# Attention with K projected for two blocks at once in the two column halves, values in groups of eight and a ring of sixteen; a two-bit search in the expert selection

## The reference, cut to what matters

```python
# attention: 8 heads, 64 + 32 columns of q and k, 64 of v
kv = (rmsnorm(c_kv, kv_norm_g) @ w_ukv).reshape(b, s, N_HEADS, QK_NOPE + V_DIM)
k = jnp.concatenate([kv[..., :QK_NOPE], broadcast(k_pe)], axis=-1)
scores = jnp.einsum('bqhd,bkhd->bhqk', qb, k)
p = jax.nn.softmax(scores, axis=-1)
o = jnp.einsum('bhqk,bkhd->bqhd', p, v)
# expert choice: each of 16 experts takes its cap best tokens of each request
aff = jax.nn.softmax(logits, axis=-1)
gates, idx = lax.top_k(aff.T, cap)          # cap = 128 (prompt), 256 (sample)
```

## Time and profile before

| | us |
|---|---|
| median of 3 runs | 4376.39 (4362.48 to 4377.37) |
| the profiled execution | 4363.99, of which span 4362.1 |
| sample attention, steady part, 600 to 1590 | 990.0, PE busy 974.8 |
| prompt attention, 1610 to 1925 | 315.0, PE busy 292.4 |
| selection, the 30 rounds, 2389.8 to 2474.0 | 84.2, DVE busy 57.7, PE 19.6 |

### The profile page before, as it was taken

The page is one execution under the profiler, slowest core; times in us unless marked ns, Lnnn a source line. Parts: engine busy times, 40 slices in busy tenths (PEclk is TensorE's granted clock), DMA queues, the critical chain, the costliest instruction groups (busy, mean ns, idle before and its releaser), DMA issues. The chain is left out here.

```text
span 4362.1 us, 53821 instructions
## 1 busy us (share of the span) xinstructions
PE 3865.6 (89%) x19385; PEld 2948.4 (68%) x19385; DVE 1752.8 (40%) x2962; ACT 1576.5 (36%) x2789; POOL 1156.4 (27%) x906
## 2 busy tenths in 40 slices
PE   7799799999999989976997259999999999999992
PEld 1799745555555534534775149999999999999991
DVE  0322144444444424345223754444444444444443
ACT  0444234444444433432222024433344333343432
POOL 0000047676767745542111130000000000000000
PEclk9899999999999989987999569999999999999996
DMA  7212300000000010024442044445444444444436
GB/s 258 99 68 74 105 4 6 7 5 8 7 8 4 6 47 10 12 91 156 150 149 95 0 136 145 145 148 159 146 144 144 144 145 154 152 144 144 144 111 250
DMA packets 296366, 428.07 MB, mean 98 GB/s; under 512 B 43558, under 2 KB 206246, under 8 KB 295050
## 3 DMA queue, kind: packets, MB, share of 16 engines
q1 hardware_dynamic: 269900, 327.41, 23.0%
q0 software_dynamic: 13824, 50.34, 5.1%
q10 hardware_dynamic: 12480, 48.24, 2.8%
HBM read 335.88 MB, written 90.06 MB: 98 GB/s over the span
## 5 line engine op out<-in xcount | busy, mean ns | idle before, releaser
L972 DVE TENSOR_REDUCE att_mx<-att_m_ps 128x1 f32<-128x512 f32 x640 | 425.3, 685 | 554.0 <-PE att_m_ps L723 554.0
L1102 POOL TENSOR_TENSOR att_acc<-att_acc,att_e 128x512 f32<-128x512 f32 x448 | 562.4, 1275 | 288.3 <-ACT att_e L917 285.6
L917 ACT ACTIVATE att_e<-att_s_ps 128x512 f32<-128x512 f32 x640 | 376.4, 595 | 614.0 <-PE att_s_ps L784 581.8
L1929 ACT ACTIVATE moe_wh<-moe_raw 128x1024 fp32r<-128x1024 f32 x384 | 373.9, 1045 | 304.7 <-DMA moe_raw<-w_up 182.0
L1976 DVE TENSOR_TENSOR moe_wl<-moe_raw,moe_wh 128x1024 fp32r<-128x1024 f32 x384 | 444.7, 1221 | 43.4 <-ACT moe_wh L1929 43.4
L1850 POOL DMA_INDIRECT s_x<-moe_ye,moe_to_add x48 | 75.8, 1580 | 1442.2 <-issue 1156.8
L1886 PE MATMUL moe_a_ps<-moe_xh,moe_wh 128*128 128x384 f32 x1024 | 350.5, 342 | 44.4 <-DVE moe_hf L2004 41.3
L1887 PE MATMUL moe_a_ps<-moe_xl,moe_wh 128*128 128x384 f32 x1024 | 347.6, 339 | 0.0
L1888 PE MATMUL moe_a_ps<-moe_xh,moe_wl 128*128 128x384 f32 x1024 | 347.6, 339 | 0.0
L1888 PE MATMUL moe_u_ps<-moe_xh,moe_wl 128*128 128x384 f32 x1024 | 342.3, 334 | 0.0
L1887 PE MATMUL moe_u_ps<-moe_xl,moe_wh 128*128 128x384 f32 x1024 | 342.2, 334 | 0.0
(11 more groups left out here) (235 smaller groups left out, 7264.1 us busy)
## 6 DMA issues: line engine op xcount, KB each, us to landing
moe_raw<-w_gate SPq DMA_DIRECT2D x64, 1024.0 KB, 5.3
moe_raw<-w_up SPq DMA_DIRECT2D x64, 1024.0 KB, 7.7
moe_raw<-w_down SPq DMA_DIRECT2D x64, 1024.0 KB, 6.7
ada_wa<-w_ada SPq DMA_DIRECT2D x12, 2048.0 KB, 9.9
s_x<-outp_x ACTq DMA_DIRECT2D x24, 512.0 KB, 5.4
s_xn<-outp_xn ACTq DMA_DIRECT2D x24, 512.0 KB, 5.9
fin_x<-s_x SPq DMA_DIRECT2D x12, 1024.0 KB, 12.1
inp_x<-x_sample SPq DMA_DIRECT2D x8, 1024.0 KB, 5.3
```

What stands on the lines that cost most here:

```text
L917: nc.scalar.activation(e[:, s % RING, :], s_ps[s % 2][:, :], ACT.Exp, scale=SCALE).then_inc(exp_done, 1)
L972: nc.vector.tensor_reduce(mx[:, u % CB, u // CB:u // CB + 1], m_ps[u % MB][:, :], AX, ALU.max).then_inc(max_part, 1)
L1102: nc.gpsimd.tensor_tensor(acc[:, b % 2, kt % 2, :], acc[:, b % 2, kt % 2, :], e[:, s % RING, :], ALU.add).then_inc(sum_done, 1)
L1929: nc.scalar.activation(wh[:, s, part, :], raw[:, s, part, :], ACT.Copy).then_inc(w_hi_done, 1)
```

## The change

Three things in attention. (1) `project_k` runs for two key blocks in one go, at every even block only: the same weights for block j into the lower and for block j+1 into the upper half of the array's columns and of the buffer. ACT then writes two pieces of `kh`, DVE two of `kl`. It stands at step 1 instead of 2, behind `values`. (2) `GROUP` is 8 instead of 4 and `RING` 16 instead of 8. (3) The prompt's step numbers of `DEN` to `OUT` now hold for the sample too, and `spread_inverses` stands right behind `values`. In selection a round settles two bits: 15 rounds, three candidates above the threshold each.

```diff
-    RING = 8
+    RING = 16
-    GROUP = 4
+    GROUP = 8
-    KSTEP = 2
-    LOW, SUM, DEN, INV, SPREAD, OUT = (3, 4, 6, 7, 9, 10) if NT == 8 else (3, 4, 8, 9, 11, 12)
+    KSTEP = 1
+    LOW, SUM, DEN, INV, SPREAD, OUT = 3, 4, 6, 7, 9, 10
...
                 for k in range(KKV):
-                    mm = nc.tensor.matmul(out[0:NOPE, :], wk[:, k0, k, :], ct_cols(KQ + k, j),
-                                          start=(k == 0), stop=(k == KKV - 1))
+                    for i in range(2):
+                        mm = nc.tensor.matmul(out[i * NOPE:(i + 1) * NOPE, :], wk[:, k0, k, :], ct_cols(KQ + k, j + i),
+                                              start=(k == 0), stop=(k == KKV - 1))
...
             for j in range(NQB):
-                if j >= 2:
-                    pe.wait_ge(k_lo_done, j - 1)
-                project_k(o_ps[j % 2], j, 0)
+                if j % 2 == 0:
+                    project_k(o_ps[j // 2], j, 0)
...
                     scores(hp, s)
-                    if kt == KSTEP and project:
...
-                        project_k(x_ps, j, 1 - h)
...
                         values(hp, group_start)
+                    finish(hp, s, SPREAD, spread_inverses)
+                    if kt == KSTEP and j % 2 == 0 and project:
...
+                        project_k(x_ps, j, 1 - h)
                     if kt == QPROJ and project:
-                        pe.wait_ge(k_lo_done, hp * NG + NQB + b + 1)
+                        pe.wait_ge(k_lo_done, hp * NG + NQB + b + 2 - j % 2)
                         project_q(1 - h, j)
                     finish(hp, s, DEN, denominators)
-                    finish(hp, s, SPREAD, spread_inverses)
...
             def k_high(src, par, j):
-                nc.scalar.activation(kh[0:NOPE, par, cols(j)], src[0:NOPE, :], ACT.Copy).then_inc(k_hi_done, 1)
+                for i in range(2):
+                    nc.scalar.activation(kh[0:NOPE, par, cols(j + i)], src[i * NOPE:(i + 1) * NOPE, :],
+                                         ACT.Copy).then_inc(k_hi_done, 1)
...
-                    if kt == KSTEP + 1 and project:
-                        dve.wait_ge(k_hi_done, hp * NG + NQB + b + 1)
-                        k_low(x_ps, 1 - h, j)
+                    if kt == KSTEP + 1 and j % 2 == 0 and project:
+                        for i in range(2):
+                            dve.wait_ge(k_hi_done, hp * NG + NQB + b + i + 1)
+                            k_low(x_ps, 1 - h, j, i)
...
-    BITS = 30
+    ROUNDS = 15
+    WAYS = 4
...
+            with dve.Fori(0, ROUNDS) as i:
+                nc.vector.tensor_tensor(cand[:].bitcast(I32),
+                                        thr[:].bitcast(I32).unsqueeze(2).broadcast_to([P, 2, WAYS, E]),
+                                        digit[:, :].unsqueeze(1).unsqueeze(3).broadcast_to([P, 2, WAYS, E]),
+                                        ALU.bitwise_or).then_inc(cand_ready, 1)
+                dve.wait_ge(cand_ready, i + 1)
+                for g, (a, b) in enumerate(groups):
+                    shape = [P, WAYS - 1, b - a, E]
+                    nc.vector.tensor_tensor(above[g][:], aff[:, a:b].unsqueeze(1).broadcast_to(shape),
+                                            cand[:, g, 1:WAYS, :].unsqueeze(2).broadcast_to(shape),
+                                            ALU.is_ge).then_inc(above_ready, 1)
+                nc.vector.tensor_scalar(digit[:, :], digit[:, :], 2, None, ALU.logical_shift_right).then_inc(digit_done, 1)
                 dve.wait_ge(counted, i + 1)
...
+                nc.vector.scalar_tensor_tensor(cand[:, :, 1:WAYS, :],
+                                               c_ps[:, 0:2 * (WAYS - 1) * E].rearrange("p (g d e) -> p g d e", g=2, e=E),
+                                               float(CAPS[1]), cand[:, :, 1:WAYS, :], ALU.is_ge,
+                                               ALU.mult).then_inc(kept, 1)
+                dve.wait_ge(kept, i + 1)
+                nc.vector.tensor_reduce(thr[:], cand[:].rearrange("p g d e -> p g e d"), AX, ALU.max).then_inc(thr_done, 1)
+                dve.wait_ge(thr_done, i + 1)
+                dve.wait_ge(digit_done, i + 1)
...
+                    pe.wait_ge(above_ready, 2 * i + g + 1)
+                    for t in range(b - a):
+                        mm = nc.tensor.matmul(c_ps[:, g * (WAYS - 1) * E:(g + 1) * (WAYS - 1) * E], weight[:, :],
+                                              above[g][:, :, t, :], start=(t == 0), stop=(t == b - a - 1))
                 mm.then_inc(counted, 1)
```

More of the change, by code:

```diff
@@ L891, in _ @@
             for j in range(NQB):
-                act.wait_ge(k_ready, j + 1)
-                k_high(o_ps[j % 2], 0, j)
+                if j % 2 == 0:
+                    act.wait_ge(k_ready, j // 2 + 1)
+                    k_high(o_ps[j // 2], 0, j)
                 act.wait_ge(q_ready, j + 1)
@@ L989, in _ @@
             for j in range(NQB):
[L990 to L991 removed]
+                if j % 2 == 0:
+                    for i in range(2):
+                        dve.wait_ge(k_hi_done, j + i + 1)
+                        k_low(o_ps[j // 2], 0, j, i)
                 dve.wait_ge(q_ready, j + 1)
@@ L1514, in selection @@
         ids = m.sb("ids", [P, TILES, 2], BF16)
-        bit = m.sb("bit", [P, 2, E], I32)
+        digit = m.sb("digit", [P, WAYS], I32)
         thr = m.sb("thr", [P, 2, E])
-        cand = m.sb("cand", [P, 2, E])
+        cand = m.sb("cand", [P, 2, WAYS, E])
+        above = [m.sb(f"above{g}", [P, WAYS - 1, b - a, E], BF16) for g, (a, b) in enumerate(groups)]
         count = m.sb("count", [P, 2, E])
@@ L1537, in selection @@
         exp_done = m.sem("exp_done")
-        bit_step = m.sem("bit_step")
+        digits_set = m.sem("digits_set")
+        cand_ready = m.sem("cand_ready")
+        above_ready = m.sem("above_ready")
+        kept = m.sem("kept")
+        thr_done = m.sem("thr_done")
+        digit_done = m.sem("digit_done")
         marked = m.sem("marked")
@@ L1603, in _ @@
                 then(nc.vector.tensor_copy(vals[:, :, :, v], ids[:, :, v].unsqueeze(2).broadcast_to([P, TILES, E])))
[L1606 removed]
+            for d in range(WAYS):
+                nc.vector.memset(digit[:, d:d + 1], d << (2 * ROUNDS - 2)).then_inc(digits_set, 1)
             then(nc.vector.memset(thr[:], 0.0))
[L1608 to L1625 removed]
@@ L1689, in _ @@
             pe.wait_ge(tabs_in, 96)
-            with pe.Fori(0, BITS) as i:
+            with pe.Fori(0, ROUNDS) as i:
                 for g, ((a, b), weight) in enumerate(zip(groups, (two, one))):
-                    pe.wait_ge(marked, 2 * i + g + 1)
-                    if g == 0:
-                        pe.wait_ge(bit_step, 5 * i + 1)
-                    mm = nc.tensor.matmul(c_ps[:, a * E:b * E], weight[:, :],
-                                          mark[:, a:b].rearrange("p t e -> p (t e)"), start=True, stop=True)
+                    pe.wait_ge(above_ready, 2 * i + g + 1)
+                    for t in range(b - a):
+                        mm = nc.tensor.matmul(c_ps[:, g * (WAYS - 1) * E:(g + 1) * (WAYS - 1) * E], weight[:, :],
+                                              above[g][:, :, t, :], start=(t == 0), stop=(t == b - a - 1))
                 mm.then_inc(counted, 1)
```

45 lines of the change are left out of this document (13 added, 32 removed).

## The result

The changed kernel takes 4256.11 us (median of 4 runs, 4253.77 to 4261.73), the kernel before 4376.12 us (4 runs, 4362.48 to 4377.37): a ratio of 0.9735, 95% interval 0.9713 to 0.9756, 2.65% faster. The forecast was 4250 us. The profiled execution took 4253.77 us with a span of 4252.0, so 110.1 us of span are gone, where the sum had 121.

A forecast was written before the change was run, and what follows sets the result against it. PE bounds attention; DVE and PE alternate in selection. Savings 89.2 + 3.6 + 28 = 121 us off the profiled 4363.99 give 4243, plus half of 12.4: 4250 us, 8-in-10 range 4228 to 4296.

The forecast's parts named there:

- Key projection (42.4): Attention, PE: 21 double key projections at 2.06 us replace 42 single ones at 2.04, saving 42.4 us.
- they do not run side by side: Rival in attention: the double projection's halves do not overlap, the 42.4 us go, total 4292 us; chance 0.07.
- Values (28.8): Attention, PE: 80 groups of values instead of 160, each with one fixed 0.36 us, saving 28.8 us.
- spreading (10.9): Sample's attention: the spreading now touches values, so 32 pieces each save 0.34 us, 10.9 us.
- Waits (net -3.6): PE's waits in attention: 18.6 us gained from old waits, new waits cost 15, net gain 3.6 us.
- 15 x 0.3: Prompt's attention: turning of the maxima waits for DVE, some 0.3 us in each of 15 blocks, 4.5 us.
- 14 x 0.5 = 7: Sample's even blocks: PE's scores of step 5 wait for step 3's exponential, 0.5 us each, 7 us.
- other engines late after the long pieces: Rival in attention: ACT and DVE fall behind, 1.0 us more in each of 48 blocks, 4298 us; chance 0.14.
- Selection (28): Selection: 15 two-bit rounds of 3.7 us, 56 us in all, saving 28 us.
- not pipelined: Rival in selection: the sixteen matmuls adding into one place do not overlap, 16 us lost, 4294 us; chance 0.07.
- The 12.4 us of which I added half: Whole kernel: the runs' median lies 12.4 us above the profiled execution; half was added to reach 4250 us.
- The stages' openings: Attention's openings: three key projections there, costed at nothing; 0 to 6 us possible.

The follow-up runs named there:

- the two later kernels: Changed kernel with sample copies spread and rounds written out: with the prompt's query projection one step later, 4284.87 us; with it in its old place, 4244.17 us.

## Why the prediction was right, point by point

**Key projection (42.4).** Right in mechanism and size. At the same place, four matmuls in two halves take 1.81 and two in one half take 1.81, so the second projection is free. Values with a double projection cost 947.62 - 941.42 - 0.71 = 5.49 (947.62 is the second matmul of the scores), less 3.77 for the values alone 1.72, and the terms have 2.06 - 0.34. Over 27 blocks of the sample, with 27 single projections before and 13 double ones after, the pieces fall from 50.2 to 23.6 us, start to start. The rival that they do not run side by side is refuted. Undoing it cost 18.4 in the sample by the projections themselves, and 9.8 in the prompt; waits that went with it are in both.

**Values (28.8) and spreading (10.9).** Right. The fixed part held at twice the length: a group of eight costs 3.77 where two of four cost 2 x 2.06. Groups of four cost 24.8 more in the sample, waits with them, and spreading alone 10.5.

**Waits (net -3.6).** The prompt's two old waits went from 15.4 to 2.7 and the new ones came where I put them: 14 waits for maxima of 3.8 (forecast 15 x 0.3; one more, of 1.3, stands ahead of the prompt's first scores and was there before with 1.6), 7 for remainders of 2.7 (forecast 3.5). A term that I had at nothing is the prompt's wait for `att_qh`: 4.5 before, 2.1 after, so 2.4 gained, and the prompt gained 34.4 where the sum has 32.9. The term that was off is the one for the sample's exponentials at step 5, "14 x 0.5 = 7". There were 16 waits, and putting the copies elsewhere gave back 11.6. The profile shows 0.4 for each and the experiment gave back 0.7: about 0.1 is the restart (as behind the spreading above, where the next matmul comes 0.34 behind the first, 937.26 - 936.92, against 0.24 in a run of scores), and where the other 0.2 was lost is not settled. Of the 5.7 missing in the sample these waits are 4.6, or 3.3 by the two later kernels. A pair of blocks became 3.6 shorter (57.5 against twice 30.55), where the prediction had 4.0. The rival *other engines late after the long pieces* names the same mechanism and prices it at 48 us above the terms: what came above them is at most 4.6, a tenth, and it came from the order of four instructions.

**Selection (28).** The round is 3.73 against 3.65 by the sum and 3.7 taken. The merge takes 0.37, not 0.29, and that is the difference. The comparisons end at 1.76 instead of 1.73, the sixteen matmuls with the gap behind them take 0.86 instead of 0.89, so that keeping starts at 2.67, where the sum put it. The sixteen start 0.040 apart, the sum's time for 48 columns. Rival *not pipelined*: refuted by 0.82 for sixteen. By the rule of the Trainium skill, page "TensorE: Matmul & The Clock Gate", section "LDWEIGHTS (loading the stationary operand)", a weight load of 128 columns is 107 ns, which laid end to end would have been 1.71 for these sixteen and a round of 4.7; the trace has 0.82 and 3.73. The trace agrees with the rule for one load (0.102 to 0.119 in these rounds) and not with laying them end to end, which was my reading: they overlap.

**What I left out.** The experts are 7.6 longer, though nothing in them changed. In both traces the stage's middle has the same work, before and after:

```profile
2612.80:4247.00 1634.20, 1590.19 (x8508) 1488.97 (x8508) 697.83 (x858) 644.13 (x981) 128.07 (x87) 0.99 0.48 145
```

```profile
2495.20:4137.00 1641.80, 1597.86 (x8510) 1496.52 (x8509) 697.58 (x858) 644.23 (x981) 128.09 (x87) 0.99 0.48 144
```

DVE, ACT and POOL are busy for the same time to 0.3 us, PE for 7.7 us more. Where this happens is seen 685 us into the stage, before and after (here a stretch of 20 us each, behind a wait of PE for DVE's `moe_hf` of 3.1 and 2.9 us):

```profile
PE moe_a_ps L1886 <- DVE moe_hf L2004: 3.1, 1, 3.1
```

```profile
PE moe_a_ps L1903 <- DVE moe_hf L2021: 2.9, 1, 2.9
```

```profile
3237.80:3257.80 20.00, 20.00 (x118) 20.00 (x117) 10.00 (x12) 9.10 (x12) 0.00 (x0) 1.00 0.65 225
```

```profile
3120.20:3140.20 20.00, 19.33 (x96) 19.34 (x97) 7.94 (x11) 6.23 (x9) 0.94 (x1) 0.83 0.79 267
```

96 matmuls instead of 118, at a clock of 0.83 instead of 1.00. By the clock records the middle has 27.3 us at half clock in the profile before and 44.4 in the one after; (44.4 - 27.3) / 2 = 8.5, close to 7.6. The changed kernel's second profile has 27.3 again and 1811.7 us, and the kernel before with the new search alone has 51.2 and 1821.6. So most of the 7.6 is a draw of the execution, and not an effect of the change; with one profile of the kernel before, a difference of the 2.4 that are left (1811.7 against 1809.2) can be neither shown nor excluded. The draw may also be most of what separates runs of one kernel (4250 to 4269 for the changed one), but unprofiled runs have no stage lengths to show it. Why some executions draw more is open. Without it the profiled gain would be 118 against 121.

**The 12.4 us of which I added half.** The medians differ by 120.0, the two profiled spans by 110.1: the profile before was a favourable draw, the one after less so. That half was a guess, no more. It left the forecast 6 too low; the sum taken from the median of the runs, 4376.4 - 121, would have been 4255. The stages' openings, which I had at nothing, are in the -0.7 of all the rest.

## What to carry to other kernels

A piece of half-width float32 matmuls between full-width ones costs a fixed 0.36 us here, at one, two and four times 512 columns, so make the pieces long and let them touch, and put two projections side by side in the halves; but what the longer pieces produce arrives at once, so spread the copies that follow over steps, in which there were 10 to 12 us here against 6.4 of visible waits. Before moving a producer one step later, add up the whole chain to its consumer: one step was worth 40 us in the prompt. In a search with a round trip per round, two bits beat one and three, and the loop itself cost 0.37 a round.

## What the runs showed of the hardware that was not expected

- The length of a wait did not tell what the clock would do: after waits of 2.9 and 3.1 us in the same place of the same stage, the granted clock was 0.83 in one profile and 1.00 in the other over the next 20 us; and in the kernel with single keys it fell to 0.74 over 20 us in which no wait was above 0.8 us.
- In the prompt with the late query projection, waits of 1.8 us in each block cost 25 us, and the stage lost 40, of which some 13 by the 26.8 us more at half clock.
- A hardware loop's turn on DVE takes 0.37 us (0.40 between merge and candidate in the loop, 0.03 written out).
- Weight loads of 128 columns in bf16, 0.102 to 0.119 us each, did not hold up matmuls of 48 columns: sixteen pairs started 0.040 us apart at a granted 0.50. With 112 columns (three bits a round) it was 0.093.
